# Stick-breaking attention rebuilt in a four-layer decoder trunk: turned q and k projections, two sets of score banks, a split softplus; and norm transposes by feature halves

## What is computed

```
z       = q @ k.T * 64**-0.5              # strictly causal: key < query
log_fail = where(strict, log_sigmoid(-z), 0)   # = -softplus(z)
between = reverse_cumsum(log_fail) - log_fail
w       = where(strict, exp(log_sigmoid(z) + between), 0)
o       = w @ v                            # then o @ w_out, added to h
```

## Time and profile before

| | |
|---|---|
| three runs | 2024.99, 2028.73, 2029.39 us (median 2028.73) |
| the profiled execution | 2025.79 us, its span in the profile 2023.8 us |
| granted TensorE clock | 0.999 of full speed |
| TensorE busy | 1982.0 us of the span |
| VectorE, ScalarE, GpSimd busy | 1166.7, 1043.1, 42.3 us |
| HBM traffic | 342.21 MB, 169 GB/s |
| stick-breaking stage, layer 0 | 207.22 to 339.24 us, 132.02 us |
| stick-breaking stage, layer 3 | 1699.0 to 1831.04 us, 132.0 us |

### The profile page before, as it was taken

How to read it: one execution, slowest core, us unless ns; L and a number is a source line. 1 busy time by engine, 2 the same in 40 slices (tenths; PEclk the granted TensorE clock), 3 DMA queues, 4 the chain that set the end, 5 groups by cost and what they waited for, 6 DMA issues and landing times.

```text
span 2023.8 us, 26278 instructions
## 1 busy us (share of the span) xinstructions
PE 1982.0 (98%) x9424; PEld 1636.1 (81%) x9424; DVE 1166.7 (58%) x1636; ACT 1043.1 (52%) x1592; POOL 42.3 (2%) x102
## 2 busy tenths in 40 slices
PE   7999999999999999999999998999999999999998
PEld 5888778888888878788888887888888888778887
DVE  4555655555655585655565557565555556646554
ACT  5444545444544465544454456554455446535443
POOL 1000000000100000000000000000000000000000
PEclk9999999999999999999999999999999999999999
DMA  6555533655556553455655544255556555425553
GB/s 209 188 186 186 171 121 103 199 185 190 176 188 188 163 186 126 146 187 187 189 185 187 187 149 138 86 167 187 187 166 208 187 187 185 147 84 166 187 187 114
DMA packets 242712, 342.21 MB, mean 169 GB/s; under 512 B 11981, under 2 KB 194906, under 8 KB 242650
## 3 DMA queue, kind: packets, MB, share of 16 engines
q1 hardware_dynamic: 242272, 341.34, 52.2%
q10 hardware_dynamic: 378, 0.02, 0.0%
HBM read 340.27 MB, written 1.05 MB: 169 GB/s over the span
## 4 chain that ended last, share of the span: by engine, by line
PE 93%; DVE 3%; ACT 2%; DMA 1%; issue 0%; SPq 0%; POOLq 0%; POOL 0%; ACTq 0%; DVEq 0%
PE psum L427 84%; PE psum L575 2%; DVE wlo L414 2%; ACT whi L400 1%; PE psum L811 1%; PE psum L458 1%; PE psum L765 1%; PE psum L831 1%; PE psum L1405 1%; PE psum L710 0%; PE psum L775 0%; DMA raw<-in_ffn_wi 0%; PE psum L834 0%; PE psum L1379 0%; PE psum L1075 0%
## 5 line engine op out<-in xcount | busy, mean ns | idle before, releaser
L414 DVE SCALAR_TENSOR_TENSOR wlo<-raw,gains,whi 128x512 fp32r<-128x512 f32 (+2 forms) x900 | 611.8, 743 | 353.7 <-ACT whi L400 353.6
L427 PE MATMUL psum<-whi,xT_hi 128*128 128x512 f32 (+1 forms) x1960 | 777.6, 397 | 18.0 <-DVE wlo L414 7.2
L427 PE MATMUL psum<-whi,xT_lo 128*128 128x512 f32 (+1 forms) x1960 | 763.1, 389 | 0.0
L427 PE MATMUL psum<-wlo,xT_hi 128*128 128x512 f32 (+1 forms) x1960 | 761.1, 388 | 0.0
L400 ACT ACTIVATE whi<-raw,gains 128x512 fp32r<-128x512 f32 (+2 forms) x900 | 570.0, 708 | 72.1 <-PE psum L427 66.1
L427 PEld LDWEIGHTS psum<-whi,xT_hi 128*128 128x128 f32 x1960 | 368.9, 188 | 93.8 <-DVE wlo L414 16.5
L427 PEld LDWEIGHTS psum<-whi,xT_lo 128*128 128x128 f32 x1960 | 368.5, 188 | 77.5
L427 PEld LDWEIGHTS psum<-wlo,xT_hi 128*128 128x128 f32 x1960 | 369.2, 188 | 70.7
L410 DVE TENSOR_TENSOR wlo<-raw,whi 128x2048 fp32r<-128x2048 f32 x100 | 229.2, 2292 | 139.6 <-ACT whi L396 139.6
L396 ACT ACTIVATE whi<-raw 128x2048 fp32r<-128x2048 f32 x100 | 191.5, 1915 | 186.6 <-PE psum L427 186.6
L427 PE MATMUL psum<-whi,hidT_hi 128*128 128x512 f32 x640 | 249.7, 390 | 0.0
(11 more groups left out here) (169 smaller groups left out, 824.8 us busy)
## 6 DMA issues: line engine op xcount, KB each, us to landing
raw<-in_ffn_wi SPq DMA_DIRECT2D x352, 512.0 KB, 4.6
raw<-in_ffn_wo SPq DMA_DIRECT2D x176, 512.0 KB, 4.2
raw<-in_sb_w_in SPq DMA_DIRECT2D x48, 512.0 KB, 4.6
raw<-in_ml_w_in SPq DMA_DIRECT2D x24, 512.0 KB, 4.6
raw<-in_sb_w_out SPq DMA_DIRECT2D x16, 512.0 KB, 4.1
raw<-in_ml_w_out SPq DMA_DIRECT2D x8, 512.0 KB, 4.1
raw<-in_mla_w_out SPq DMA_DIRECT2D x8, 512.0 KB, 4.2
raw<-in_mla_w_in SPq DMA_DIRECT2D x4, 512.0 KB, 4.2
```

Of the source, the lines that this page charges most:

```text
L414: last = dve.scalar_tensor_tensor(wlo[:, slot, r], raw[:, slot, r], gain_col(p.gain + k), hi[:, r], op0=ALU.mult, op1=ALU.subtract)
L427: m = pe.matmul(dst, a, b[:, slot, cols], start=first and n == 0, stop=last and n == 2)
```

## The change

- **Turned projections.** For q and k the weights are the stationary operand (128 columns at a time) and the 256 tokens move, so that q and k come out transposed. A piece is 48 matmuls of 256 columns, where it was 24 of 512. `transposes`, their copies on ScalarE and `y_fill` are gone. `rstd` now has to run along the columns: GpSimd makes two diagonal matrices, one fp32 product with ones (`rows_pe`) spreads them, ScalarE copies them to `rows`, and VectorE multiplies by `rows` as it brings a half block to SBUF.
- **Banks.** All six blocks use the pair 4 and 3 (`SB_PAIR`); the scores of groups 0 and 2 use banks 0 to 2, those of 1 and 3 banks 5 to 7.
- **Triangle.** softplus is split into `sp_hi` (ScalarE) and `sp_lo` (VectorE), and the triangle and the ones are fp32r: two rounds of fp32r matmuls where there was one of fp32.
- **Values.** v is stationary (128 keys x 64 features), the weights w move (256 or 128 columns); even heads land in partitions 0 to 63, odd ones in 64 to 127. The result is already transposed: no copy to `y`, no `y_fill`.
- **Norm transposes.** `GROUPS` runs over the token halves first; the four transposes use banks 0, 1, 2 and 7 and no longer wait for each other's reads; two of them stand ahead of the last product group.

The diff, cut to its core:

```diff
-GROUPS = [(t, nh) for t in range(TT) for nh in range(HALVES)]
+GROUPS = [(t, nh) for nh in range(HALVES) for t in range(TT)]
+FILL_BANK = (0, 1, 2, 7)
 UP = ((0, 1), (4, 5))
...
+sp_hi = sb("sp_hi", [P, 3 * NCOL], F32R)
+sp_lo = sb("sp_lo", [P, 3 * NCOL], F32R)
+ones = sb("ones", [P, P])
+diag = sb("diag", [P, TT, P])
+rows = sb("rows", [P, SEQ])
...
         pe.wait_ge(h_done, 4 * (j - 1) + g + 1)
     else:
         pe.wait_ge(x_loaded, 16 * TT)
-    if q >= 2:
-        pe.wait_ge(tr_read, q - 1)
-    fill_pe(pe, h, 7 - g % 2, *GROUPS[g])
+    fill_pe(pe, h, FILL_BANK[g], *GROUPS[g])
 
 def norm_split(eng, j, g):
     t, nh = GROUPS[g]
-    fill_split(eng, norm_fill0(j) + g, 7 - g % 2, t, 4 * nh)
+    fill_split(eng, norm_fill0(j) + g, FILL_BANK[g], t, 4 * nh)
 
 def norm_act(act, j):
...
-                act.wait_ge(h_done, 4 * (j - 1) + 2 * t + 2)
+                act.wait_ge(h_done, 4 * (j - 1) + 3 + t)
             act.activation(y[:, t, :], h[:, t, :], ACT.Square, accum_out=ssq[:, t:t + 1]).then_inc(ssq_done, 1)
...
     norm_split(dve, j, 0)
+    norm_split(dve, j, 1)
     if j:
         residual(3)
-    norm_split(dve, j, 1)
-    if j == 0:
+    else:
         converts(dve, convert_dve, 0)
     norm_split(dve, j, 2)
...
     pe.wait_ge(lo_ready, s.piece0 + 1)
-    for t in range(TT):
-        if t:
-            norm_fill(pe, j, 3)
-        pe.wait_ge(tr_read, q + 2 * t + (2 if whole else 1))
-        m = project(pe, slot, t, UP[0][t], 0, p.tiles, p.cols, True, whole)
-        if whole and t == 0:
-            m.then_inc(proj_done, 1)
+    if s.kind == "sb":
+        pe.wait_ge(tr_read, q + 2)
+        m = turned_half(pe, s, 0, 0, 0)
+        norm_fill(pe, j, 3)
+        m = turned_half(pe, s, 0, 0, 1)
+    else:
+        for t in range(TT):
+            if t:
+                norm_fill(pe, j, 3)
+            pe.wait_ge(tr_read, q + t + 1)
+            m = project(pe, slot, t, UP[0][t], 0, p.tiles, p.cols, True, False)
     m.then_inc(piece_used, 1)
 
...
             norm_fill(pe, j, 0)
+            norm_fill(pe, j, 1)
     if j < len(subs):
...
+def rows_pe(pe, s, bank):
+    pe.wait_ge(diag_done, s.rows0 + 1)
+    pe.matmul(psum[:, bank, 0:SEQ], ones[:, :], diag[:, :, :].rearrange("p t n -> p (t n)"), start=True,
+              stop=True).then_inc(rows_done, 1)
+
+def rows_act(act, s, bank):
+    act.wait_ge(rows_done, s.rows0 + 1)
+    act.activation(rows[:, :], psum[:, bank, 0:SEQ], ACT.Copy).then_inc(rows_ready, 1)
 
...
-SB_Z, SB_AV = (0, 0, 0, 4), (3, 7, 7, 7)
+SB_Z, SB_AV, SB_PAIR = (0, 5, 0, 5), (0, 1, 5, 6), (4, 3)
+
+def turned_half(pe, s, b, n, side):
+
+    m, k0 = s.piece0 + n, 4 * (n % 2)
+    for blk in range(2):
+        dst = psum[:, SB_PAIR[side], blk * SEQ:(blk + 1) * SEQ]
+        for k in range(4):
+            c = k * NCOL + (2 * side + blk) * P
+            for a, (w, v) in enumerate(((whi, xT_hi), (wlo, xT_hi), (whi, xT_lo))):
+                i = pe.matmul(dst, w[:, m % RING, c:c + P], v[:, k0 + k, :],
+                              start=k0 + k == 0 and a == 0 and blk == 0, stop=k0 + k == KD - 1 and a == 2,
+                              skip_group_check=True)
+    return i
...
 def sb_pe(pe, s):
+    def turned(n, between=None):
+        b = n // 2
+        pe.wait_ge(lo_ready, s.piece0 + n + 1)
+        for side in range(2):
+            if n % 2 == 0:
+                pe.wait_ge(proj_read, 2 * (s.block0 + b) - 1 + side)
+            i = turned_half(pe, s, b, n, side)
+            if n % 2 and side == 0:
+                i.then_inc(proj_done, 1)
+            if side == 0 and between:
+                between()
+        i.then_inc(piece_used, 1)
+
+    def plain(n):
+        b = n // 2
+        pe.wait_ge(lo_ready, s.piece0 + n + 1)
+        for t in range(TT):
+            if n % 2 == 0:
+                pe.wait_ge(proj_read, 2 * (s.block0 + b) - 1 + t)
+            i = project(pe, (s.piece0 + n) % RING, t, SB_PAIR[t], 4 * (n % 2), 4, NCOL, n % 2 == 0, n % 2 == 1)
...
-            pe.wait_ge(proj_read, 2 * (s.block0 + 6))
-        elif g:
-            pe.wait_ge(w_done, 4 * s.inst + g)
+        pe.wait_ge(proj_read, 2 * (s.block0 + (2 if g < 2 else 4)))
+        if g >= 2:
+            pe.wait_ge(w_done, 4 * s.inst + g - 1)
         mask_pe(pe, 0, SB_Z[g])
         scores_pe(pe, g, SB_Z[g], kT, qT, False).then_inc(z_done, 1)
...
     def remainder(g):
-        bank, sp3 = SB_Z[g], sb_sp[:, g % 2, :]
-        pe.wait_ge(sp_done, 4 * s.inst + g + 1)
-        for b in range(3):
-            pe.matmul(psum[:, bank + b, :], neg_tri[:, :], sp3[:, b * NCOL:(b + 1) * NCOL], start=False,
-                      stop=b == 2, skip_group_check=True)
-        for b in range(2):
-            pe.matmul(psum[:, bank + b, P:SEQ], neg_ones[:, :], sp3[:, KT1[b]:KT1[b] + P],
-                      start=False, stop=True, skip_group_check=True)
-        i = pe.matmul(psum[:, bank + 2, :].rearrange("p (a n) -> p a n", a=2)[:, :, P:SEQ], neg_ones[:, :],
-                      sp3[:, 0:2 * NCOL].rearrange("p (a n) -> p a n", a=2)[:, :, KT1[2]:KT1[2] + P],
-                      start=False, stop=True, skip_group_check=True)
+        bank = SB_Z[g]
+        pe.wait_ge(sp_lo_done, 4 * s.inst + g + 1)
+        for sp3 in (sp_hi, sp_lo):
+            for b in range(3):
+                pe.matmul(psum[:, bank + b, :], neg_tri[:, :], sp3[:, b * NCOL:(b + 1) * NCOL], start=False,
+                          stop=b == 2, skip_group_check=True)
+            for b in range(2):
+                pe.matmul(psum[:, bank + b, P:SEQ], neg_ones[:, :], sp3[:, KT1[b]:KT1[b] + P],
+                          start=False, stop=True, skip_group_check=True)
+            i = pe.matmul(psum[:, bank + 2, :].rearrange("p (a n) -> p a n", a=2)[:, :, P:SEQ], neg_ones[:, :],
+                          sp3[:, 0:2 * NCOL].rearrange("p (a n) -> p a n", a=2)[:, :, KT1[2]:KT1[2] + P],
+                          start=False, stop=True, skip_group_check=True)
         i.then_inc(r_done, 1)
 
...
     def values(g):
+
+        pe.wait_ge(w_done, 4 * s.inst + (3 if g < 2 else 4))
         pe.wait_ge(proj_read, 2 * (s.block0 + (5 if g < 2 else 6)))
+        for p in range(2):
+            for kt in range(TT):
+                for odd in range(2):
+                    hh = 2 * p + odd
+                    c, w0 = (GROUP * g + hh) * 64, (KT0, KT1)[kt][hh]
+                    i = pe.matmul(psum[64 * odd:64 * odd + 64, SB_AV[g], p * SEQ + kt * P:(p + 1) * SEQ],
+                                  v_sb[:, kt, c:c + 64], sb_e[:, g, w0:w0 + SEQ - kt * P],
+                                  start=p == 0 and kt == 0, stop=kt == 1, skip_group_check=True)
+        i.then_inc(tr_done, 1)
...
```

More of the change, by code:

```diff
@@ L300, in trunk @@
         subs, static = [], {}
-        pieces, blocks, fills, plains, ffns, sbs, ys = 0, 0, TT * HALVES, 0, 0, 0, 0
+        pieces, blocks, fills, plains, ffns, sbs, ys, row_sets = 0, 0, TT * HALVES, 0, 0, 0, 0, 0
         for i in range(DEPTH):
@@ L475, in norm_fill @@
         def norm_fill(pe, j, g):
-            q = norm_fill0(j) + g
             if j:
@@ L849, in sb_pe @@
+                i.then_inc(tr_done, 1)
+            pe.wait_ge(tr_read, norm_fill0(s.index) + 4)
+            turned(1, lambda: rows_pe(pe, s, 0))
+            turned(2)
+            turned(3)
+            turned(4)
             scores(0)
-            piece(6)
-            transposes(2)
-            piece(7)
+            turned(5)
+            scores(1)
+            turned(6)
+            turned(7)
             remainder(0)
-            piece(8)
-            transposes(3)
-            scores(1)
@@ L857, in sb_pe @@
-            piece(9)
-            piece(10)
-            remainder(1)
+            plain(8)
+            scores(2)
+            remainder(1)
+            plain(9)
+            scores(3)
+            plain(10)
+            remainder(2)
+            plain(11)
             values(0)
-            scores(2)
             values(1)
-            piece(11)
-            y_fill(pe, s, 0, 3)
-            y_fill(pe, s, 1, 7)
-            remainder(2)
-            scores(3)
-            pe.wait_ge(w_done, 4 * s.inst + 3)
+            remainder(3)
@@ L869, in sb_pe @@
+            pe.wait_ge(tr_read, s.norm_fill0 - 4 + 2)
+            pe.wait_ge(proj_read, 2 * (s.block0 + 6))
             out_piece(pe, s, 0)
             values(2)
-            remainder(3)
-            y_fill(pe, s, 2, 7)
+            values(3)
             out_piece(pe, s, 1)
-            values(3)
-            out_piece(pe, s, 2, {1: lambda: y_fill(pe, s, 3, 7)})
+            out_piece(pe, s, 2)
             out_piece(pe, s, 3)
         def sb_act(act, s, link):
-            def copies(b):
-                pairs = slice(0, 4) if b < 2 else slice(4, 8)
-                for t in range(TT):
-                    act.wait_ge(plain_T, s.plain0 + 2 * b + t + 1)
-                    bank, cols = psum[:, 6 + t, :].rearrange("p (j n) -> p j n", j=4), slice(t * P, (t + 1) * P)
```

(52 more changed lines are left out.)

170 lines of the change are left out of this document (83 added, 87 removed).

## The result

The changed kernel takes 1998.12 us (median of 4 runs, 1995.39 to 2001.18), the kernel before 2028.9 us (4 runs, 2024.99 to 2029.39). The ratio is 0.9853, with an interval of 0.983 to 0.9876. The prediction, 2002 us, was 3.9 us too long.

The account below looks back on a forecast made before the run. TensorE, busy 98% of the span, was taken as the bound; terms summed to -12.8 us a stage, -25.6 in all, giving 2000.2 or 2003.1 us by starting point. Forecast 2002 us, range 1993 to 2013.

Parts of the forecast that it names:

- Turned projections: q and k pieces of the stick-breaking stage: 0.1205 us a matmul, eight pieces cost +2.6 us a stage.
- rival 3: Short matmuls don't hide their weight loads: +41 us a stage, about 2085 us; chance 0.03.
- Removed work and holes: TensorE in the stick-breaking stage: transposes gone, -3.2 and -1.6 us; two waits gone, -3.1 us.
- Triangle: Softplus remainders as two fp32r rounds, 2.05 us instead of 3.45: four times 1.4, -5.6 us a stage.
- Rival 4: The split triangle isn't faster, fp32r running at fp32's pace: +4.9 us eight times, 2041 us; chance 0.02.
- Values: Value products: 1.6 us a group, within 1.3 to 2.6, instead of 2.62: -4.1 us a stage.
- Rival 1: Column halves don't overlap, values stay at 2.6 us: +4.1 us a stage, 2010 us; chance 0.25.
- The new waits: TensorE waits for shared banks at two block boundaries, 1.0 and 0.7 us: +1.8 us a stage in all.
- The 0.1 for the second norm split: At the stage's start, TensorE can stand 0.1 us, since a turned matmul takes all tokens.
- Rival 2: Shared bank pair holds TensorE at boundaries: 8 us a stage instead of 1.8, 2014 us; half, 2008; chance 0.13.
- Cover: Input of `rows_pe` ready by 214.3 at most, TensorE arrives at 216.4: hidden; uncovered, up to 1 us.
- The norm part: Norm transposes between SwiGLU steps and in the tail: no gain; the end 0, at worst 0.3 us later.

Follow-up runs that it names:

- e1: The changed kernel with the triangle back in plain fp32 on the unsplit softplus: 2008.8 us, ratio 0.9905 to the kernel before.
- e8: The changed kernel with 128 stationary columns instead of 64 in the values' matmuls, so it doesn't compute the attention: 2009.05 us, one time.
- e4: The changed kernel with evacuation 0.1 ahead of piece 3's split and evacuations 3.0 and 3.1 ahead of piece 9's on VectorE: 1996.12 us.
- e7: The changed kernel with VectorE's splits of pieces 5 and 6 each ahead of an evacuation of block 1: 2004.5 us, ratio 0.9893 to the kernel before.
- e3: The kernel before with only the norm part: token halves first, four banks, two transposes ahead of the last product group: 2027.91 us, ratio 1.0002.
- e9: The kernel of e1 with each 512-column triangle matmul made as two of 64 stationary columns, one per column half: 2007.33 us, ratio 0.9902.
- e2: The changed kernel with each group's value matmuls reordered, four for even heads, then four for odd: 1999.57 us, ratio 0.9865 to the kernel before.
- e10: The changed kernel with two groups' value matmuls in one order, eight for partitions 0 to 63, then eight for 64 to 127: 2004.31 us, one time.

## Why the prediction was right

*Turned projections.* Right: 0.1200 us a matmul for the 0.1205 of the line through 384 and 512 columns, +2.5 for +2.6. The loads stay hidden although the record of a load lasts longer (0.19 us) than the matmul's pace; rival 3 is out. The rule of the Trainium skill (TensorE: Matmul & The Clock Gate, Part 3) that only loads for other rows overlap isn't borne out by these 48 matmuls in 5.8 us either.

*Removed work and holes.* The transposes gave 3.2 and 1.5 us and the holes 3.1, as read from the earlier trace rows.

*Triangle.* Right to 0.25 us a stage. The two of 128 columns and the one of 256 behind them take 0.34 us together, as forecast (0.22 and 0.12). One by one they start 0.056, 0.112 and 0.172 us apart (260.41, 260.47, 260.58, 260.75), while their loads start 0.11 us apart (260.41, 260.52, 260.63): the pace of the loads holds, with the first load already done beside the 512 columns ahead. A round is 1.04 for 1.02. Rival 4 is out. Run e1 shows the term: 5.2 us a stage.

*Values.* The step that was mis-sized: 1.6 us a group was taken, by the nearest row, and 1.375 came. The true price was near the lower end of the bounds, two streams fully side by side: four times 0.213 and four times 0.107 are 1.28, the rest is at the seams. The upper end, 2.6 without overlap, is what run e8 measures (2.58). Rival 1 had its price right and its answer wrong. The Trainium skill's sentence that different tiles can load and compute in parallel (TensorEngine Tiling (Array Packing), Key Properties) agrees with the record starts: 32 records at 16 start times.

*The new waits.* Right in both places and in what is queued ahead, too long in both: the step that was mis-sized next to the values. The first took 0.7 us instead of 1.0 (start to start; 0.55 of it is the wait of block 1's second half on the row at 223.04), the second 0.23 instead of 0.7. The 0.1 for the second norm split came too, ahead of the point from which the stage is counted. Run e4 takes both away and finds 1.1 us a stage. Rival 2 didn't come, because only two evacuations that have a split ahead of them end after TensorE asks for their bank; run e7 shows that one more such place costs 4.8 us a stage, not the 2 us that the rival counted. At that price five boundaries, twice, would come to 48 us, more than the change gained; only the one was tried.

*Not in the sum.* The slow first matmuls behind the holes and the transposes went with them, 0.5 us a stage.

*Cover.* GpSimd's `diag` ended at 214.45, 0.15 us after the latest moment forecast, and `rows_pe` ran at 216.15: hidden, with 1.7 us to spare. The norm part gave nothing and cost 0.7 us at the end of the program (run e3), where 0, at worst 0.3, was forecast: the forecast had looked at the order of the groups, and not at GpSimd's `mean_sq`, which takes 0.9 us beside VectorE's write of `y`.

*Sum.* -14.9 for -12.8 a stage; values 0.95, waits 0.9, first matmuls 0.5 and turned pieces 0.1 on one side, the triangle's 0.25 and the transposes' 0.1 on the other. Taken twice from 2028.9 that is 1999.1, and 1998.1 came. Every term of the sum had its sign and its mechanism right; the sizes were off. That twice 14.9 meets the difference of the medians within 1 us is partly luck, since the clock in the MLA stage alone moves an execution by up to 5 us.

What stays open: one set of score banks beside the turned projections wasn't tried, so what the second set brings by itself isn't known. The turned projections and the new form of the values weren't run apart from each other either; their terms are read from the starts in one trace. Why the clock drops in the MLA stage in some executions and not in others isn't known either; the waits ahead of the drop are the same in both cases.

## What to carry to other kernels

When TensorE is the bound, price a new form of matmul by its columns at the clock and a constant read from neighbouring rows, and price products of 64 stationary columns as two streams side by side if they alternate between the column halves, one by one. If banks are shared between a block and the next, place each evacuation ahead of the weight splits in the queue: what stands behind a split also stands behind the other engine's half of that split, and a hole of 2.7 us cost 1.4 us more by the slow records that followed it. To judge a gain of a few us, compare stages in traces, since a stage repeats to 0.05 us where the total scatters by 5.

## What the runs showed of the hardware

- fp32 records stream at 256 columns in 0.213 us with 64 stationary columns as with 128: 0.43 for 512 columns with 64 stationary columns (run e9) and with 128. An overall pace of records hides this: 32 records in 3.57 us in run e2 were partly single and partly in pairs. Starts of records tell it, sums don't.
- Products for the two column halves overlap only where they stand close in the queue: the other half's matmuls started up to two matmuls ahead of their turn (runs e2 and e10). 2.75 us alternating, 3.57 in blocks of four, 4.75 in blocks of eight, 5.16 with none.
- A hole of 2.7 us was followed by 3 us at the lower of the two clock levels (run e7, granted clock 0.51), while the 1.7 us hole of before and the 0.6 us one now were followed by none. The length of a hole doesn't decide it alone: in the MLA stage waits of 1.5 and 2.3 us were followed by a granted clock of 0.50 in one execution and of 1.00 in another.
- Weight loads of 128 columns start 0.11 us apart at the least, in the 160 column stretch and in the triangle's short matmuls. Two of 128 columns behind one of 512 take 0.17 us, since one load runs beside the long one; the next of 256 takes 0.17 instead of 0.12. Read alone, the 0.17 for two looks like a pace of 0.085 that a longer run of them wouldn't keep (an estimate; none ran).
- An operation of GpSimd on a 128x1 tile (`mean_sq`) took 0.19 us with VectorE idle and 0.92 while VectorE wrote `y` (runs before and e3); that VectorE is the cause isn't shown by more than this.
